# Mixture-of-experts items of 32 slots on four column groups of TensorE, in place of 64 slots on two

## The reference

```python
logits = (xf @ w_router + b_router)
top_val, top_idx = lax.top_k(logits, TOP_K)          # 4 of 32 experts
top_w = softmax(top_val)
for e in range(N_EXPERTS):
    hh = xf @ w_expert_in[e] + b_expert_in[e]         # 1024 -> 2048
    gate = minimum(hh[:, :1024], 7); lin = clip(hh[:, 1024:], -7, 7)
    act = (lin + 1) * gate * sigmoid(1.702 * gate)
    y += comb[:, e:e+1] * (act @ w_expert_out[e] + b_expert_out[e])   # 1024 -> 1024
```

## Time and profile before

| | |
|---|---|
| median of 3 runs | 1615.55 us (1614.3 to 1619.29) |
| profiled execution | 1610.57 us, its span 1608.8 us |
| granted clock of PE, mean | 0.957 |
| PE busy | 1480.3 us (92%) |
| DVE, ACT, POOL busy | 308.3, 206.3, 156.4 us |
| DMA moved | 533.56 MB, mean 332 GB/s |
| in the last item PE's output layer ends | 1582.9 us |

### The profile page before, as it was taken

The page is one execution under the profiler, slowest core; times in us unless marked ns, Lnnn a source line. Parts: engine busy times, 40 slices in busy tenths (PEclk is TensorE's granted clock), DMA queues, the critical chain, the costliest instruction groups (busy, mean ns, idle before and its releaser), DMA issues.

```text
span 1608.8 us, 17919 instructions
## 1 busy us (share of the span) xinstructions
PE 1480.3 (92%) x6906; PEld 733.0 (46%) x6907; DVE 308.3 (19%) x593; ACT 206.3 (13%) x385; POOL 156.4 (10%) x221
## 2 busy tenths in 40 slices
PE   6999999988999899999998998998998998999993
PEld 3777887656877533333333333333333332333331
DVE  1022114324211411212111112112112112112113
ACT  3000213533000210101001000000001000000001
POOL 0230000100620001000000000100000000000000
PEclk9999999999999899999999999999999999999996
DMA  9767634997355465679999999999999999999991
GB/s 363 292 245 279 216 131 175 369 408 275 86 184 210 157 240 214 249 300 426 422 418 422 423 423 424 419 413 426 425 414 421 411 425 417 423 409 422 419 414 57
DMA packets 78617, 533.56 MB, mean 332 GB/s; under 512 B 7561, under 2 KB 8673, under 8 KB 51729
## 3 DMA queue, kind: packets, MB, share of 16 engines
q1 hardware_dynamic: 67330, 503.47, 76.6%
q0 software_dynamic: 10864, 28.72, 5.5%
q10 hardware_dynamic: 391, 0.93, 0.2%
HBM read 507.62 MB, written 30.50 MB: 334 GB/s over the span
## 4 chain that ended last, share of the span: by engine, by line
PE 61%; DMA 33%; DVE 3%; SPq 1%; issue 1%; ACT 1%; DVEq 0%; ACTq 0%; POOL 0%; POOLq 0%
DMA ring<-in_w_expert_in_dram 26%; PE ps L924 15%; PE ps L945 15%; PE ps L748 13%; PE ps L497 3%; DMA vslot<-in_state_ret_dram 3%; DMA out_dram<-vslot 2%; PE ps L841 2%; PE ps L791 2%; DMA ring<-in_w_ada_dram 2%; PE ps L806 2%; PE ps L799 2%; PE ps L888 2%; PE ps L896 1%; PE ps L544 1%; DMA vslot<-in_w_up_ret_dram 1%
## 5 line engine op out<-in xcount | busy, mean ns | idle before, releaser
L924 PE MATMUL ps<-ring,xgT 128*64 128x512 f32 x1632 | 405.4, 642 | 41.9 <-DMA ring<-in_w_expert_in_dram 41.4
L748 PE MATMUL ps<-hT,ring 128*128 128x264 f32 x1152 | 269.6, 392 | 4.5 <-ACT hT L1021 2.3
L924 PEld LDWEIGHTS ps<-ring,xgT 128*64 128x64 f32 x1632 | 120.6, 147 | 303.5 <-issue 248.2
L748 PEld LDWEIGHTS ps<-hT,ring 128*128 128x128 f32 x1152 | 219.2, 192 | 59.5 <-issue 20.0
L945 PE MATMUL ps<-moe_ring,actT 128*64 128x512 f32 x1088 | 242.6, 598 | 0.4 <-ACT actT L1165 0.4
L945 PEld LDWEIGHTS ps<-moe_ring,actT 128*64 128x64 f32 x1088 | 78.0, 137 | 140.4 <-issue 135.6
L1486 DVE COPY xg<-ps 128x512 f32<-128x512 f32 x35 | 24.2, 691 | 610.6 <-PE ps L888 610.6
L924 PE MATMUL ps<-moe_ring,xgT 128*64 128x512 f32 x544 | 122.5, 592 | 0.0
L888 PE MATMUL ps<-rows,picked 128*64 128x512 f32 (+1 forms) x420 | 101.4, 599 | 1.7 <-ACT x_rows L1149 1.7
L1161 ACT ACTIVATE glu_s<-glu_g 128x512 f32<-128x512 f32 x34 | 21.4, 629 | 447.3 <-DVE glu_g L1498 447.3
L924 PEld LDWEIGHTS ps<-moe_ring,xgT 128*64 128x64 f32 x544 | 39.1, 137 | 77.7 <-issue 77.7
(11 more groups left out here) (273 smaller groups left out, 1065.4 us busy)
## 6 DMA issues: line engine op xcount, KB each, us to landing
ring<-in_w_expert_in_dram SPq DMA_DIRECT2D x96, 2048.0 KB, 16.6
moe_ring<-in_w_expert_out_dram SPq DMA_DIRECT2D x64, 2048.0 KB, 10.7
moe_ring<-in_w_expert_in_dram SPq DMA_DIRECT2D x32, 2048.0 KB, 17.8
ring<-in_w_in_dram SPq DMA_DIRECT2D x18, 2048.0 KB, 11.1
ring<-in_w_ada_dram SPq DMA_DIRECT2D x12, 2048.0 KB, 9.3
ring<-in_state_ret_dram SPq DMA_DIRECT2D x8, 1024.0 KB, 11.4
vslot<-in_state_ret_dram SPq DMA_DIRECT2D x8, 1024.0 KB, 12.8
out_dram<-ring POOLq DMA_DIRECT2D x8, 1024.0 KB, 9.2
```

The source lines that it names most:

```text
L748: mm = nc.tensor.matmul(ps[:, j, 0:T], ring[s][:, k, j * P:(j + 1) * P], hT[:, k, :], start=(k == 0), stop=(k == KC - 1))
L924: mm = nc.tensor.matmul(side(bank, g), xgT[:, 2 * j + a, :], w[:, a, c * COL:(c + 1) * COL], start=False, stop=(j == 3 and a == 1))
```

## The change

SLOTS becomes 32, and SIDES = 128 / 32 = 4 column groups take the place of two. Side g is now the partitions 32g to 32g+31.
- Hidden layer: the four groups hold the four 512-column quarters of the 2048 hidden columns, all in one bank: gate in the partitions 0 to 63, lin in 64 to 127. DVE and ACT work on 64 partitions, 512 columns each.
- Gather and output layer: each of the four groups takes 256 of the 1024 columns. xg and ostage are 128 x 256 in place of 128 x 512. There are two transposes for the gathered rows (four before) and four for the activation, of 64 partitions.
- The scatter adds rows of 1 KB; a token has four of them in place of two of 2 KB.
- PE's order: hidden(1) comes ahead of outward(q - 1), and pick(q + 1) goes to the end of the item, behind turn_gathered.
- POOL writes bias_out within the scatter, between the copy of the slot numbers and the indirect DMA, in place of behind the landed scatter.
- The list of items is longer: with the token counts above 49 items. Experts 1 and 2 have three, the experts 3, 4, 5, 6, 11, 12, 15, 17, 18, 20, 23, 25 and 30 two, the other 17 one.

```diff
@@ -52,7 +52,10 @@
...
-SLOTS = 64
+SLOTS = 32
+SIDES = P // SLOTS
+QUARTER = D // SIDES
+OVERS = 8
...
@@ -99,8 +102,8 @@
...
-    put("slotval", 2 * token - SKIP)
-    put("over", np.tile(SLOTS * np.arange(1, 5), (P, 1)))
+    put("slotval", SIDES * token - SKIP)
+    put("over", np.tile(SLOTS * np.arange(1, OVERS + 1), (P, 1)))
@@ -198,16 +201,16 @@
...
         xs = at("xs", [P, KC, T], top[0])
-        xg = new("xg", [P, COL])
-        xgT = new("xgT", [P, KC, SLOTS])
-        actT = new("actT", [P, KC, SLOTS])
+        xg = new("xg", [P, QUARTER])
+        xgT = new("xgT", [P, 2, SIDES * SLOTS])
+        actT = new("actT", [P, 4, 2 * SLOTS])
         onehot = at("onehot", [P, 3, TOPK, E], top[0])
-        act = new("act", [P, COL])
+        act = new("act", [2 * SLOTS, COL])
         product = at("product", [P, 3, TOPK, E], top[0])
-        glu_g = new("glu_g", [P, COL])
-        glu_l = new("glu_l", [P, COL])
-        glu_s = new("glu_s", [P, COL])
-        ostage = new("ostage", [P, COL])
+        glu_g = new("glu_g", [2 * SLOTS, COL])
+        glu_l = new("glu_l", [2 * SLOTS, COL])
+        glu_s = new("glu_s", [2 * SLOTS, COL])
+        ostage = new("ostage", [P, QUARTER])
         assert top[0] <= h_at
...
@@ -884,8 +887,8 @@
...
                 for t, (t0, n) in enumerate(TILES):
-                    for g in range(2):
-                        mm = nc.tensor.matmul(ps[SLOTS * g:SLOTS * (g + 1), 6, :], picked[0:n, t, 0:SLOTS], rows[0:n, t, g * COL:(g + 1) * COL],
+                    for g in range(SIDES):
+                        mm = nc.tensor.matmul(side(6, g)[:, 0:QUARTER], picked[0:n, t, 0:SLOTS], rows[0:n, t, g * QUARTER:(g + 1) * QUARTER],
                                               start=(t == 0), stop=(t == 2))
@@ -898,9 +901,8 @@
...
                 pe.wait_ge(xg_taken, q + 1)
-                for c in range(2):
-                    for a in range(2):
-                        mm = turn(ps[:, 3, (2 * c + a) * P:(2 * c + a + 1) * P], xg[:, 2 * P * c:2 * P * (c + 1)].rearrange("s (p a) -> s a p", a=2)[:, a, :])
+                for a in range(2):
+                    mm = turn(ps[:, 3, a * P:(a + 1) * P], xg[:].rearrange("s (p a) -> s a p", a=2)[:, a, :])
                 mm.then_inc(xg_turned, 1)
@@ -909,40 +911,37 @@
...
                 pe.wait_ge(hidden_taken, 2 * q + 2)
-                for bank in range(2):
-                    for g in range(2):
-                        c = 2 * bank + g
-                        nc.tensor.matmul(side(bank, g), bias_sel[:], bsplit[:, c * COL:(c + 1) * COL], start=True, stop=False)
+                for g in range(SIDES):
+                    nc.tensor.matmul(side(0, g), bias_sel[:], bsplit[:, g * COL:(g + 1) * COL], start=True, stop=False)
...
                 for a in range(2):
-                    for bank in range(2):
-                        for g in range(2):
-                            c = 2 * bank + g
-                            mm = nc.tensor.matmul(side(bank, g), xgT[:, 2 * j + a, :], w[:, a, c * COL:(c + 1) * COL],
-                                                  start=False, stop=(j == 3 and a == 1))
+                    for g in range(SIDES):
+                        mm = nc.tensor.matmul(side(0, g), xgT[:, a, j * SLOTS:(j + 1) * SLOTS], w[:, a, g * COL:(g + 1) * COL],
+                                              start=False, stop=(j == 3 and a == 1))
                 mm.then_inc(chunk_used[j], 1)
...
                 pe.wait_ge(act_ready, q + 1)
+                pe.sem_inc(pe_pace, 1)
                 for a in range(4):
-                    mm = turn(ps[:, 4, a * P:(a + 1) * P], act[:].rearrange("s (p a) -> s a p", a=4)[:, a, :])
+                    mm = turn(ps[:, 4, 2 * SLOTS * a:2 * SLOTS * (a + 1)], act[:].rearrange("s (p a) -> s a p", a=4)[:, a, :])
                 mm.then_inc(act_turned, 1)
...
                 pe.wait_ge(eo_taken, q + 1)
-                for g in range(2):
-                    nc.tensor.matmul(side(2, g), bias_out[:], bsplit_out[:, g * COL:(g + 1) * COL], start=True, stop=False)
+                for g in range(SIDES):
+                    nc.tensor.matmul(side(2, g)[:, 0:QUARTER], bias_out[:], bsplit_out[:, g * QUARTER:(g + 1) * QUARTER], start=True, stop=False)
                 pe.wait_ge(act_taken, q + 1)
...
                     for a in range(4):
-                        for g in range(2):
-                            mm = nc.tensor.matmul(side(2, g), actT[:, 4 * h + a, :], w[:, a, g * COL:(g + 1) * COL],
+                        for g in range(SIDES):
+                            mm = nc.tensor.matmul(side(2, g)[:, 0:QUARTER], actT[:, a, h * SLOTS:(h + 1) * SLOTS], w[:, a, g * QUARTER:(g + 1) * QUARTER],
                                                   start=False, stop=(h == 1 and a == 3))
@@ -968,14 +967,14 @@
...
                 turn_hidden(q - 1)
-                pe.wait_ge(slots_taken, SLOT_STEPS * q + SLOT_STEPS)
-                pick(q + 1, after)
+                hidden(1, e)
                 outward(q - 1, before)
-                hidden(1, e)
                 gather(q + 1)
...
                 turn_gathered(q + 1)
+                pe.wait_ge(slots_taken, SLOT_STEPS * q + SLOT_STEPS)
+                pick(q + 1, after)
             last = pe.value_load(item_i[0:1, bass.ds(items - 1, 1)], min_val=0, max_val=E - 1)
@@ -1154,7 +1153,7 @@
...
                 act_e.wait_ge(xg_turned, q + 1)
-                nc.scalar.copy(xgT[:].rearrange("p (g k) s -> p k g s", g=2), ps[:, 3, :].rearrange("p (k g s) -> p k g s", k=4, g=2)).then_inc(xgT_ready, 1)
+                nc.scalar.copy(xgT[:].rearrange("p a s -> p (a s)"), ps[:, 3, 0:2 * P]).then_inc(xgT_ready, 1)
@@ -1162,13 +1161,13 @@
...
                 act_e.wait_ge(act_turned, q + 1)
-                nc.scalar.copy(actT[:].rearrange("p (g a) s -> p a g s", g=2), ps[:, 4, :].rearrange("p (a g s) -> p a g s", a=4, g=2)).then_inc(act_taken, 1)
+                nc.scalar.copy(actT[:].rearrange("p a s -> p (a s)"), ps[:, 4, 0:8 * SLOTS]).then_inc(act_taken, 1)
...
                 act_e.wait_ge(slots_taken, SLOT_STEPS * q + SLOT_STEPS)
-                nc.scalar.activation(ostage[:], ps[:, 2, :], ACT.Copy, scale=slots_w[:, bass.ds(q, 1)]).then_inc(eo_taken, 1)
+                nc.scalar.activation(ostage[:], ps[:, 2, 0:QUARTER], ACT.Copy, scale=slots_w[:, bass.ds(q, 1)]).then_inc(eo_taken, 1)
@@ -1483,7 +1482,7 @@
...
                 dve.wait_ge(xg_ready, q + 1)
-                cp(xg[:], ps[:, 6, :]).then_inc(xg_taken, 1)
+                cp(xg[:], ps[:, 6, 0:QUARTER]).then_inc(xg_taken, 1)
@@ -1495,8 +1494,8 @@
...
                 dve.wait_ge(chunk_used[3], q + 1)
-                ts(glu_g[:], ps[:, 0, :], LIMIT, None, ALU.min).then_inc(glu_ready, 1)
-                ts(glu_l[:], ps[:, 1, :], LIMIT, -LIMIT, ALU.min, ALU.max).then_inc(glu_step, 1)
+                ts(glu_g[:], ps[0:2 * SLOTS, 0, :], LIMIT, None, ALU.min).then_inc(glu_ready, 1)
+                ts(glu_l[:], ps[2 * SLOTS:P, 0, :], LIMIT, -LIMIT, ALU.min, ALU.max).then_inc(glu_step, 1)
                 dve.wait_ge(glu_ready, q + 1)
@@ -1600,21 +1599,23 @@
...
             items = pool.value_load(cum_i[0:1, E - 1:E], min_val=E, max_val=ITEMS)
-            out_halves = moe_rows.rearrange("t (h n) -> (t h) n", h=2)
+            out_halves = moe_rows.rearrange("t (h n) -> (t h) n", h=SIDES)
...
-            def scatter(q):
+            def scatter(q, here):
                 pool.wait_ge(eo_taken, q + 2)
...
                 cp(slot_u[:], slots_u[:, bass.ds(q, 1)]).then_inc(slot_u_ready, 1)
+                if here is not None:
+                    bias_column(bias_out, here, out_bias_ready)
                 pool.wait_ge(slot_u_ready, q + 1)
...
                                         in_=ostage[:], in_offset=None,
-                                        bounds_check=2 * T - 1, oob_is_err=False, compute_op=ALU.add).then_inc(eo_stored, 16)
+                                        bounds_check=SIDES * T - 1, oob_is_err=False, compute_op=ALU.add).then_inc(eo_stored, 16)
                 pool.wait_ge(eo_stored, q * 16 + 16)
@@ -1630,11 +1631,8 @@
...
                 bias_column(bias_sel, after, bias_sel_ready)
-                scatter(q - 1)
-                pool.wait_ge(chunk_used[4], q)
-                pool.sem_inc(pool_pace, 1)
-                bias_column(bias_out, here, out_bias_ready)
-            scatter(items - 1)
+                scatter(q - 1, here)
+            scatter(items - 1, None)
```

More of the change, by code:

```diff
@@ L64 @@
 _at = 0
-for _name, _w in [("ident", P), ("iota", P), ("selc", T), ("iota3", 3 * E), ("slotval", 3), ("over", 4), ("eye96", 36),
+for _name, _w in [("ident", P), ("iota", P), ("selc", T), ("iota3", 3 * E), ("slotval", 3), ("over", 8), ("eye96", 36),
                   ("ones", P), ("upper", P), ("cos", T), ("sin", T), ("decay", HEADS * TP), ("kdecay", 2 * HEADS),
@@ L219, in trunk_kernel @@
         top[0] = v_at + 12544
-        over_n = new("over_n", [E, 4])
```

(1 more changed line is left out.)

## The result

The changed kernel takes 1576.9 us (median of 4 runs, 1573.4 to 1579.4); the kernel before took 1615.6 beside it (4 runs). The ratio is 0.976, with a 95% interval of 0.974 to 0.978: 2.4% faster. The forecast was 1576. The profiled execution has a span of 1577.6 us, took 1579.36 in all, and shows a mean granted clock of 0.906, where 0.957 stood before. Medians and ratios in this document are of fast executions alone; one execution of the changed kernel in the slow state, of 3039.5 us, is in none of them.

What follows compares the result with a forecast made beforehand. Loads bound the kernel from 740 us on; before that they starved, 52.5 us in all. Last landing 1537.4, end 1566.5, plus 3 for the scatter gave a 1569.5 us span and a median of 1576; range 1560 to 1612.

Steps and rivals of the forecast that it cites:

- The item: PE's time for one item, bias to bias: 14.7 us, against 27.36 before.
- The holes: Time in which loads starve at experts 1 and 2: 12.5 and 13.9 us, together 26.4 where 52.5 were.
- the sum: Span added up by the loads: 1566.5 plus 3 for the scatter, 1569.5 us, 39 less than 1608.8.
- The first release: First freeing of a chunk buffer in item 0: at 571.2 us, 3.8 us earlier than before.
- The forecast's 3 us for the scatter: Cost of adding 4224 rows of 1 KB for 2112 of 2 KB on the DMA engines: 3 us.
- The threshold: Item time above which experts with two items starve the loads: 15.12 us, half of 30.24 us per expert.
- a little over the threshold: Rival: items of 15.2 to 16.3 us cost 5 to 25 us more, 1580 to 1600; chance 0.17.
- The bias column: POOL's bias_out, if still behind the scatter, would come about when the output layer wants it; no size given.
- Short pairs bound by issue: Rival: output and gather pairs pace at 80 to 122 ns, not 54; 1620 to 1640, up to 1759 us; chance 0.12.
- Scatter by row: Rival: scatter time goes by row, not bytes, 24 us on the DMA engines, 1597 us in all; chance 0.06.
- No effect: Rival: loads saturate anyway and the holes stay as large, 1612 to 1619 us; chance 0.05.
- The clock: PE's granted clock falls well below 0.95; 0 to 22 us in experts of two items, taken as 0.

Runs made afterwards that it cites:

- out_first: The changed kernel with the second layer, outward(q - 1), put back ahead of hidden(1); 1596.4 us, 0.989 of the kernel before.
- pad_small: The changed kernel with the first third of each gather done twice, order untouched; 1577.9 us, 0.978 of the kernel before.
- gather_twice: The changed kernel with the gather's 24 matmuls done twice in each item; 1611.6 us, 0.998 of the kernel before.
- pick_early: The changed kernel with the pick put back ahead of hidden(1); 1609.5 us, 0.997 of the kernel before.
- after_again: The changed kernel itself, unedited, run again in a later batch; 1573.7 us, 0.976 of the kernel before.
- order_only: The kernel before (64 slots, two groups) with only pick at the item's end, hidden(1) ahead of outward, bias_out ahead of the scatter; 1655.6 us.
- one_clamp: The changed kernel with one DVE clamp on 128 partitions for two, and ACT's xgT copy ahead of the sigmoid; 1575.8 us, again 1571.2.

## Why the prediction was right

**The item.** Forecast 14.7 us, measured 14.78. Biases 0.23 for 0.35, chunk 0 1.84 for 1.87, turns 0.63 for 0.5, chunk 1 1.74 for 1.71, output bias 0.11 for 0.2, output layer 3.45 for 3.46, gather 1.55 for 1.54, the last two chunks 3.57 for 3.55, the gap behind them 1.66 for 1.52. The step that carried this was to take four groups as halving a chunk, by the one row that showed the shape.

**The holes.** Forecast 12.5 and 13.9 us. By the share of the windows, 0.67 of 18 us and 0.75 of 17 us stood idle: 12.1 and 12.8.

**What was mis-sized.** The span came out at 1577.6 where the sum said 1569.5. The releases show where the 8.1 us lie. The first release was forecast for 571.2 and came at 575.23, +4.0. I compare the starts with those of before. Item 0's steps come 1.0 us later already ahead of the stage; between there and the first chunk 1.3 of the 2.1 us that I had taken off were not won; and the chunk took 3.64 us instead of 1.92 (1.7). The window 571 to 575 shows why: the granted clock is 0.50, the 1.2 GHz level. In out_first, where these steps are the same, that chunk ran at full clock:

```profile
568.54 1.92 PE L922 MATMUL ps<-ring,xgT 128*32 128x512 f32 x16
```

Its release came at 570.53, near the 571.2 of the forecast.

Expert 2's chunk 0 was forecast to be free at 613.9 and was at 620.00, so 2.1 us more were lost. Expert 1's second chunk came late and ran at the lower clock, 3.41 us to the next start for the sum's 1.71:

```profile
589.28 3.60 PE L922 MATMUL ps<-ring,xgT 128*32 128x512 f32 x16 [1.90 <-DMA ring<-in_w_expert_in_dram]
```

Expert 3's was forecast for 658.0 and came at 665.31: +7.3 up to there. From that release to the last landing, the end of this row of the chain, it took 882.8 us:

```profile
1534.21 13.93 DMA moe_ring<-in_w_expert_out_dram
```

The sum has 879.4 and 3 for the scatter, so +0.4. From the last landing to the end it took 29.5 us for 29.1, +0.4 again.

So the terms that were mis-sized are the first release and expert 1's first item. Of their 6.1 us, 3.4 are two chunks at the lower clock, on which the prediction put nothing there; the rest is steps ahead of the first chunk that start later or win less than I took off, and of these the cause stays open. The forecast's 3 us for the scatter fit the landings. By packet times it looks too small: a 1 KB row takes 0.123 us where a 2 KB row took 0.18, so the change added 4224 x 0.123 - 2112 x 0.18 = 139 us of engine time, 8.7 on each engine. The stretch of the last 29 experts has room for 3.4 us of this; why the rest doesn't show there stays open. That the median still agrees is luck in part: the sum added 6.5 us for what lay around the span and above the profiled execution, and this time the profiled execution was not below the median.

**The threshold.** Forecast 15.12 us an item, measured 15.35 (half of 30.7), raised by the scatter's share of the engines. The item lies 0.6 us below it. pad_small at 15.20 costs 1 to 4 us, gather_twice at 16.34 costs 35. The rival "a little over the threshold" was priced at 5 to 25 us for items of 15.2 to 16.3, too low, since I thought that experts of one item give time back. The runs showed no such return: pick_early lost 29.2 us behind expert 3's release, more than the 22.4 of 13 x (2T - 30.7). The loads run at their rate in the experts of one item already, and lost transfer time can't be caught up there; that reading is argued, not tried by itself.

**The bias column.** I wrote that, behind the scatter, it would come "at about the same time as the output layer wants it". It comes 1.5 to 1.9 us late, and that is worth the whole gain. The term was cheap in us and dear by where it lay.

**What I did not see.** That hidden(1)'s place matters through the buffers' order, not through the copy that it covers. By the item's time out_first should cost 3 us; it costs 19.5, and on 64 slots the move that helps here costs 41. Nothing in my sum held that term; it came out right since the change has the order that is good at this item's length.

**The rivals.** Short pairs bound by issue: ruled out, at 54 ns a pair. (Its items were added up 0.3 us too long: with the pairs as priced they are 20.4 and 16.7 us, not 20.7 and 17.0.) The Trainium skill (TensorE: Matmul & The Clock Gate, Back-to-back issue gap) gives about 81 ns for sustained pairs of 128 columns; with 32-column weights and 256 columns on four groups the trace shows less, and the measurement decides. Scatter by row: 8.7 us of its 24 by packet times, and at most 3.4 by the landings. No effect: ruled out by the ratio. The clock fell as forecast, to 0.906, and cost where PE was on the path: at the first release, at expert 1's second chunk, and in the last output layer, where 3.64 us stand for the 1.93 of after_again; the forecast had 3.5 for that.

## What to carry to other kernels

Where one ring of buffers is loaded by an in-order queue, keep the books by release: a stage's price is a threshold (here 2T against 30.7 us per expert). An item of 15.20 us, under it, costs 1 to 4 us in all; one of 16.2 or 16.3, 1 us over it, costs 33 to 35. Read how far each step lies from the threshold before you call a wait of 1.5 us small. The order of consumers has to be the order of loads: work that waits for a late chunk must not stand ahead of work that could free an early one, and, when the item is long, must not stand behind so much that the queue's last buffers come free late; so an order that helps at one size (here 32 slots) can cost 41 us at another. Compare the first release before you compare two kernels that are a few us apart.

## What the runs showed of the hardware

- Four column groups with 32-column weights run fully beside each other down to 256 columns: 54 ns for a pair of weight load and matmul, 16 chunk matmuls in 1.92 us against 3.65 on two groups.
- A full DMA share is not a full rate: 391 GB/s at a share of 1.01 in pick_early against 419 at 1.02 in the changed kernel, in the same stretch. What differs is how late the loads are released: 12.6 MB in the 32.4 us between two releases are 388 GB/s. Why the packets then take longer stays open.
- An accumulating row takes 0.123 us of packet time at 1 KB and 0.18 at 2 KB, as with a fixed part of about 0.07 us and the rest by bytes. By the landings of 20 experts with 562 tokens it costs 0.12 us at 1 KB and 0.22 at 2 KB, nearly by bytes alone; this is an estimate that takes 29.51 us an expert as the bare loads of both kernels.
- A wait of 2.7 to 2.8 us for a load is followed by a slow chunk in order_only: 5.34, 5.08 and 6.61 us for 3.65 at three experts in a row, the first at a granted clock of 0.67.
- The first release comes at 575.23 and 575.06 in two profiled executions of the changed kernel, and at 570.27 and 570.21 in two of one_clamp, with nearly the same instructions up to there. The granted clock around the first chunk (571 to 575 us) is 0.50 and 0.59 in the two of the changed kernel; in one_clamp (568 to 570.2) it is 1.00 in both. What decides it was not tried.
